# Changing the order of the narrow products behind four input norms

## The reference

```
h = rms_norm(x, gain)            # second block: * (1 + scale) + shift
p = h @ w_in                     # 1024 x several thousand columns
```

## Time and profile before

| what | value |
|---|---|
| runs | 3591.50, 3592.83, 3595.72 us |
| span of the profiled execution | 3591.6 us |
| TensorE matmul busy | 3524.8 us, 98% |
| VectorE busy | 2133.1 us, 59% |
| ScalarE busy | 1397.9 us, 39% |
| DMA mean | 101 GB/s |

### The profile page before, as it was taken

One profiled execution on the slowest core, in us unless ns is written; L12 is line 12 of the kernel. 1 busy time (PEld: TensorE's weight loads), 2 busy tenths in 40 slices (PEclk: granted clock), 3 DMA queues, 4 the chain that ended last, 5 costly groups with the idle time before them and its releaser, 6 DMA issues. The chain is left out here.

```text
span 3591.6 us, 53181 instructions
## 1 busy us (share of the span) xinstructions
PE 3524.8 (98%) x21547; PEld 2899.6 (81%) x21547; DVE 2133.1 (59%) x2993; ACT 1397.9 (39%) x1599; POOL 0.2 (0%) x4
## 2 busy tenths in 40 slices
PE   8999999999999999999999999999999999999998
PEld 6778888887877788888878878988888778888887
DVE  6888465876368884558763657653233667652233
ACT  6455433343255544333432434233222443332223
POOL 0000000000000000000000000000000000000000
PEclk9999999999999999999999999999999999999999
DMA  4222223554232222226542331132222330122322
GB/s 130 80 78 64 81 84 105 201 187 163 85 87 84 72 70 75 90 98 207 187 164 82 96 129 49 49 108 93 95 94 85 104 128 27 61 106 96 102 94 70
DMA packets 273303, 364.38 MB, mean 101 GB/s; under 512 B 22636, under 2 KB 218976, under 8 KB 271840
## 3 DMA queue, kind: packets, MB, share of 16 engines
q1 hardware_dynamic: 247856, 311.34, 26.9%
q10 hardware_dynamic: 25264, 50.43, 4.0%
HBM read 351.79 MB, written 9.96 MB: 101 GB/s over the span
## 5 line engine op out<-in xcount | busy, mean ns | idle before, releaser
L249 PE MATMUL banks<-act_hi,w_hi 128*128 128x512 f32 x4064 | 1607.4, 396 | 23.5 <-issue 6.3
L251 PE MATMUL banks<-act_hi,w_lo 128*128 128x512 f32 x4064 | 1584.3, 390 | 0.0
L250 PE MATMUL banks<-act_lo,w_hi 128*128 128x512 f32 x4064 | 1582.8, 389 | 0.0
L171 DVE TENSOR_TENSOR w_lo<-w_raw,w_hi 128x2048 fp32r<-128x2048 f32 (+1 forms) x280 | 629.2, 2247 | 636.2 <-ACT w_hi L165 632.1
L249 PEld LDWEIGHTS banks<-act_hi,w_hi 128*128 128x128 f32 x4064 | 762.8, 188 | 220.0 <-issue 46.8
L251 PEld LDWEIGHTS banks<-act_hi,w_lo 128*128 128x128 f32 x4064 | 762.2, 188 | 162.3
L250 PEld LDWEIGHTS banks<-act_lo,w_hi 128*128 128x128 f32 x4064 | 762.9, 188 | 157.6 <-issue 3.8
L165 ACT ACTIVATE w_hi<-w_raw 128x2048 fp32r<-128x2048 f32 (+1 forms) x280 | 526.6, 1881 | 910.0 <-PE banks L251 846.6
L2115 DVE SCALAR_TENSOR_TENSOR arena<-arena,small 128x512 f32<-128x512 f32 x168 | 126.3, 752 | 12.9
L249 PE MATMUL banks<-w_hi,act_hi 128*128 128x256 f32 x384 | 111.0, 289 | 3.6 <-DVE w_lo L171 3.6
L250 PE MATMUL banks<-w_lo,act_hi 128*128 128x256 f32 x384 | 109.3, 285 | 0.0
(11 more groups left out here) (387 smaller groups left out, 3428.4 us busy)
## 6 DMA issues: line engine op xcount, KB each, us to landing
w_raw<-in_w_in SPq DMA_DIRECT2D x98, 1024.0 KB, 5.4
w_raw<-in_ffn_up SPq DMA_DIRECT2D x48, 1024.0 KB, 5.3
arena<-in_ada_w ACTq DMA_DIRECT2D x24, 2048.0 KB, 8.1
w_raw<-in_w_gu SPq DMA_DIRECT2D x44, 1024.0 KB, 5.1
w_raw<-in_ffn_down SPq DMA_DIRECT2D x24, 1024.0 KB, 4.9
w_raw<-in_w_down SPq DMA_DIRECT2D x20, 1024.0 KB, 4.9
w_raw<-in_w_out SPq DMA_DIRECT2D x16, 1024.0 KB, 4.9
w_raw<-in_w_branch SPq DMA_DIRECT2D x12, 1024.0 KB, 5.1
```

The source lines that it names most:

```text
L171: self.core.nc.vector.tensor_tensor(view(self.lo[:, s]), view(self.raw[:, s]), view(self.hi[:, s]).bitcast(FP32), ALU.subtract)\
L249: nc.tensor.matmul(out, wh, ah, start=first, stop=False)
L250: nc.tensor.matmul(out, wh, al, start=False, stop=False)
L251: return nc.tensor.matmul(out, wl, ah, start=False, stop=last)
```

## The change

`misc` makes its two banks together, and `lora` its three: tile after tile, first the products with the high activation half for every bank, then the wait for the low half, then the products with it. The count of matmuls is the same. The completion counts `tile`, `done` are raised on the last matmul of each bank, which now all stand at the end of the one loop. In the first layer, whose low halves are read from banks 1 and 3 themselves, two low halves are waited for first.

```diff
-            for s in (0, 1):
-                if um:
-                    pe.wait_ge(ring.bank_free[2 * s + 1], um)
-                for k in range(KD):
-                    if s == 0:
-                        pe.wait_ge(n.lo, k + 1)
-                    wh, wl = (b[:, s].rearrange("p (k n) -> p k n", k=8)[:, k, 0:128] for b in (ring.hi, ring.lo))
-                    last = three_pass(nc, ps[:, 2 * s + 1, :], (wh, wl), (self.hi[:, k, :], self.lo[:, k, :]),
-                                      k == 0, k == KD - 1)
-                last.then_inc(ring.done[s], 1)
+            halves = [[b[:, s].rearrange("p (k n) -> p k n", k=8)[:, :, 0:128] for b in (ring.hi, ring.lo)]
+                      for s in (0, 1)]
+            if um:
+                pe.wait_ge(ring.bank_free[1], um)
+                pe.wait_ge(ring.bank_free[3], um)
+            if raw:
+                pe.wait_ge(n.lo, 2)
+            for k in range(KD):
+                pe.wait_ge(n.hi, k + 1)
+                for s, (wh, wl) in enumerate(halves):
+                    out = ps[:, 2 * s + 1, :]
+                    nc.tensor.matmul(out, wh[:, k], self.hi[:, k, :], start=(k == 0), stop=False)
+                    nc.tensor.matmul(out, wl[:, k], self.hi[:, k, :], start=False, stop=False)
+                pe.wait_ge(n.lo, k + 1)
+                for s, (wh, _) in enumerate(halves):
+                    last = nc.tensor.matmul(ps[:, 2 * s + 1, :], wh[:, k], self.lo[:, k, :], start=False,
+                                            stop=(k == KD - 1))
+                    if k == KD - 1:
+                        last.then_inc(ring.done[s], 1)
...
+            first = [(ps[:, b, :], [v[:, :, b * P:b * P + P] for v in wide_w]) for b in (0, 1)]
+            first.append((ps[0:64, 2, :], [v[:, :, 0:64] for v in narrow_w]))
             for k in range(KD):
+                pe.wait_ge(n.hi, k + 1)
+                for out, (wh, wl) in first:
+                    nc.tensor.matmul(out, wh[:, k], self.hi[:, k, :], start=(k == 0), stop=False)
+                    nc.tensor.matmul(out, wl[:, k], self.hi[:, k, :], start=False, stop=False)
                 pe.wait_ge(n.lo, k + 1)
-                for b in (0, 1):
-                    last = three_pass(nc, ps[:, b, :], [v[:, k, b * P:b * P + P] for v in wide_w],
-                                      (self.hi[:, k, :], self.lo[:, k, :]), k == 0, k == KD - 1)
+                for b, (out, (wh, _)) in enumerate(first):
+                    last = nc.tensor.matmul(out, wh[:, k], self.lo[:, k, :], start=False, stop=(k == KD - 1))
                     if k == KD - 1:
-                        last.then_inc((ring.tile[0], ring.done[0])[b], 1)
-            for k in range(KD):
-                last = three_pass(nc, ps[0:64, 2, :], [v[:, k, 0:64] for v in narrow_w],
-                                  (self.hi[:, k, :], self.lo[:, k, :]), k == 0, k == KD - 1)
-            last.then_inc(ring.tile[1], 1)
+                        last.then_inc((ring.tile[0], ring.done[0], ring.tile[1])[b], 1)
             pe.drain().then_inc(ring.done[1], 1)
```

## The result

Four runs of the changed kernel took 3612.76 to 3615.95 us, median 3614.55 us; four runs of the kernel before, on the same chip, had a median of 3593.36 us. The ratio is 1.006, with a 95% interval of 1.0048 to 1.0072: slower by 21.2 us. The profiled execution has a span of 3614.2 us (3615.95 us as a run), 22.6 us over the span before. Forecast were 3611.7 us and +18.9 us; the time lies in the range.

A forecast was written before the change was run, and what follows sets the result against it. TensorE's matmuls, filling 98% of the span, were taken as the bound. Layer terms 4.95 + 0.1 + 3.9 + 3.9 plus 6.0 for the clock gave +18.9 us on 3592.8, so 3611.7 us; 8-in-10 range 3605 to 3616.5.

The forecast's parts named there:

- (1): First layer, behind misc: ScalarE's rounding L165 starts at about 40.0 and not 34.15.
- (2): Before aqi: TensorE idle 4 us in first layer, nearly 6 in second, whose aqi stays about 7.1 us behind eighth low half.
- (3): Third and fourth layers: TensorE idle nearly 6 us before pool, released by VectorE's L171.
- (4): Behind the four pauses the granted clock is 0.50; taken as 1.5 us each, +6 us, range 0 to 12.
- (5): TensorE's waits for L529 and L531, 3.4 and 2.3 us before, are nearly gone.
- Rival B: Turnover laid bare at the places, but the clock mostly holds in the pauses: 3605.7 us; chance 0.17.
- rival C: Next slot ready when the merged loop ends, turnover under 0.3 us: faster, -8.7 us, 3584.1 us; chance 0.02.
- five terms of the forecast: First to fourth layer +4.95, +0.1, +3.9 and +3.9 us, and the clock +6.0 us.
- Rival D: Later VectorE-bound stretch takes in first and second layer's loss: 3603.6 us, chance 0.07; full cancelling to within 0.2%, 0.04.
- rival E: Later rounding delays a second item, or clock stays low through a second stretch: 5 us more, 3617 us; chance 0.06.
- A: The forecast itself: slot turnover laid bare at three places, clock falls in the pauses: 3611.7 us; chance 0.62.
- Rival F: Clock swings in the merged loops through the bank order: +48 us, 3660 us; chance 0.02.

The follow-up runs named there:

- late_release: Kernel before with its old product order, only slot 0's release (in lora bank 0's too) moved behind slot 1's products: 3622.45 us, ratio 1.0084.
- misc_only: Kernel before with only the misc half of the change (layers one and two): 3600.36 us, ratio 1.0025.
- filled: Changed kernel with 16 (first layer) or 24 matmuls that nobody reads put into each of the four pauses: 3606.05 us, ratio 1.0044.
- round_first: Changed kernel, but behind lora slot 0's rounding goes ahead of the bank copies and its low half ahead of VectorE's shifts: 3607.87 us, ratio 1.0046.
- lora_only: Kernel before with only the lora half of the change (layers three and four): 3604.91 us, ratio 1.0037.
- merged_low_first: Changed kernel with its merged loops, but each tile waits for its low half first: 3613.55 us, ratio 1.0064.

## Why the prediction was right

Its rows (1) to (5) point by point.

(1) L165 in the first layer was forecast for about 40.0 instead of 34.15, that is 12.6 us behind the start of the low halves. It came at 39.12 - 26.41 = 12.7. `late_release` shows that the release is what sets it.

(2) Idle before `aqi`: 4.04 us in the first layer (4 forecast), 5.78 in the second (nearly 6). The second's distance behind the eighth low half was forecast at 7.1 us and was 7.72. **This term was mis-sized**: +0.67 where the step had +0.1. The step took the loop to be paced by the norm to its end. In after the fillers ahead of it ran at half clock (the window from 1022 to 1024), and L488's ended about when the first matmul of `misc` started, at 1024.44. The loop's first two distances were still 0.43 us instead of 0.23. No wait stands in this loop, so TensorE was behind the norm from its start, and ScalarE's rounding behind the loop came 1.81 us after the eighth low half (1035.94 against 1034.13) instead of 1.12. In `misc_only`, where the window was granted 0.66, the place cost 0.11 us; in `filled` and `round_first` it was 7.16 and 7.15. The working was right for a loop that starts in time; whether it does hangs on the clock in a stretch that the change does not touch.

```profile
1022.00:1024.00 2.00, 2.00 (x8) 1.59 (x7) 1.87 (x4) 1.27 (x2) 0.00 (x0) 0.66 0.71 250
```

(That is `misc_only`.) The fourth layer's +4.51 us against 3.9 is the same. `lora` starts at 2814.30 behind the last filler, though its first high half was there at about 2812.85 + 0.69 = 2813.54: 0.76 us late, where the step took 0.14. The fillers, then ScalarE's first two high halves:

```profile
2811.68 2.78 PE L488 MATMUL banks<-w_hi 128*128 128x512 f32 x6
```

```profile
2812.85 1.38 ACT L513 ACTIVATE act_hi<-arena,small 128x512 fp32r<-128x512 f32 x2 [3.58 <-DVE arena L536]
```

In `lora_only` six of these fillers took 1.82 us instead of 2.78, TensorE waited for the first high half, and the place cost 4.03 us:

```profile
2804.24 1.82 PE L488 MATMUL banks<-w_hi 128*128 128x512 f32 x6
2806.28 0.47 PE L2408 MATMUL banks<-act_hi,w_hi 128*128 128x512 f32 x1 [0.22 <-ACT act_hi L513]
```

(3) `pool` waited 5.67 and 5.74 us for L171. The copy of bank 0 to the end of L171 is 2041.95 - 2035.96 = 5.99 us, against the 6.00 that the step carried over. Third layer +3.98, forecast +3.9.

(4) The clock was 0.50 behind the pauses. Its size was low. Twelve matmul distances from TensorE's return took 2.84 us in the first layer of before (41.00 to the row below), 2.82 to 2.84 in its other three, and, after, 4.42 (45.04 to 49.46), 4.79 (from 1041.85), 4.79 (from 2042.01) and 5.04 us (from 2836.77). The kernel before:

```profile
43.84 0.39 PE L249 MATMUL banks<-act_hi,w_hi 128*128 128x512 f32 x1
```

That is 1.6, 1.95, 1.95 and 2.2 us lost, **7.7 us against the 6.0** of the step, and `filled` gives 5 to 7 by another way. The step took the loss of one pause, over eight distances at the earlier trace rows, for all four; behind the pauses of after the slow stretch was longer, up to the eleventh distance in the fourth layer. (the earlier trace rows do not carry the clock behind the pause of 2.01 us; the window from 170 to 172 was granted 0.50.) Rival B (the clock holds) is out.

(5) The waits for L529 and L531 are gone, and it did not help: rival C is out, since the turnover takes 6 us and not 0.3.

The sum: places 14.2, clock 7.7, and 1.0 back for an opening that was that much earlier in this one execution, 20.9 of the 22.6 us of span. The 1.7 us that are left are the balance of larger differences between the places: +1.7 from the first to the second, -1.3, -0.4, and +1.6 behind the fourth. Differences of that size are also seen between executions of the same program: from the first layer's eighth low half to the second's `lora_only` took 995.4 us and before 994.0, and the two are the same up to there. So the sum closes no better than to some 2 us, and what these differences are was not isolated. All five terms of the forecast measured more than it had, three of them clearly, by 0.6, 0.6 and 1.7 us; none made up for another. That the total lies within 2.3 us of the forecast shows little by itself, as the interval is 4.3 us to a side: the terms are confirmed by the rows, not by the total. Rival D (the first block's loss given back by stretches bound by VectorE) would have left `misc_only` near before; it has +7.5 us, with an interval from 5.4 to 12.6, for 5.2 us in its places and 3.0 of clock. Of rival E nothing but more of A's own terms is seen, the late coming to two loops among them: the waits for L171 less the two pauses are 5.9 us, as before, so no second slot came late. Rival F (a clock that swings in the merged loops) is out as well: 48 matmuls in the first layer took 39.09 - 28.08 = 11.0 us, as in the earlier trace rows.

## What to carry to other kernels

A loop order that removes waits at its head can pay for them at its tail: before products of two buffers are merged into one loop, ask what is released when the first buffer's last product is done, and what lay over that turnover. Here the removal of 5.7 us of waits was paid for with four pauses of 4 to 6 us; the same high-first order with the second buffer's products left behind is level with the kernel before. A pause of TensorE is to be priced at its length plus what the clock takes after it, here 7.7 us behind pauses of 21.2 us. The places cost 14.2 us and not 21.2, as some of the moved products are now made in the waits of the norm or start earlier.

## What the runs showed of the hardware that was not expected

Matmuls whose result nobody reads, put into a pause, held the granted clock at 1.00 (window 1034 to 1037 of `filled`) and, for 88 added matmuls, the kernel took 8.0 us less of 3614 us by the medians, 5 to 7 of them by the clock. No place got longer by more than 0.01 us.

A pause cost 1.6 us of clock behind 4.04 us of idle, 1.95 behind 5.67 and behind 5.78, and 2.2 behind 5.74: pauses of one length do not cost the same. In `misc_only`, the same program as after up to there, the second layer's pause of 5.78 us cost only 1.4 us (twelve distances of 4.24 us); in `merged_low_first` the fourth layer's 5.74 us cost 2.4 (5.28 us). And the second norm's fillers, L488, were granted 0.66 in `misc_only` and 0.50 in after, which are the same program up to there (six of them took 2.58 and 2.91 us), and with that a place moved by 0.6 us.

The merged loops go round two or three banks in each tile, and 48 matmuls of the first layer took 11.0 us in either order. The Trainium skill, page "TensorE: Matmul & The Clock Gate", section "A second HAM failure mode: psum-queue depth-cycling", tells of a kernel that went round the banks in each iteration and whose clock swung through small pauses. No run here shows that.
